# Moving the delta-rule preparation of a gated-DeltaNet layer into the input projection of the same layer

## Chip, cores and metric

The kernel runs on one core of a Trainium2 chip. It is one program in Bass, one launch. The metric is the device time of one execution in microseconds; lower is better. Everything is float32 except the operands of the large projections, which are split into a high and a low float32r part and multiplied in three passes.

## What is computed

A decoder of two layers on 2048 tokens, width 1024. Layer 1 is a gated DeltaNet (8 heads of 128), layer 2 an attention with forget gates (16 heads of 64) over one shared K/V stream. The change is in layer 1 alone:

```python
proj = h @ w_in                                  # 3072 columns q,k,v; 1024 z; 8 a; 8 b
qkv = silu(causal_conv4(qkv, conv_w))
q, k = l2_norm(q), l2_norm(k)                    # per head
beta = sigmoid(b);  g = -exp(a_log) * softplus(a + dt_bias)
g_c = cumsum(g) within a chunk
decay = exp(tril(g_c[i] - g_c[j]))
a_strict = tril((k*beta) @ k.T * decay, -1)      # Gram product of k with k
qk = (q @ k.T) * decay                           # Gram product of q with k
u, w = solve((a_strict + I), [v*beta, k*beta*exp(g_c)])
# then a scan over the chunks with a 128x128 state per head
```

The kernel takes chunks of 128 tokens (16 chunks). Only the 32x32 diagonal blocks of `a_strict + I` are inverted by elimination; larger blocks are joined by matmuls in the scan.

## The kernel before

The program is a row of stages. Each stage (`Stage`) has its own tensors and semaphores and ends with a barrier of all engines; results pass through DRAM. Names carry the stage's prefix: `st` (modulation vectors and first norm), `pa` (projection of layer 1), `da` (delta-rule preparation), `dr` (the scan), `oa` (output projection), `pk`, `pb` (projections of layer 2), `at` (attention), `ob` (output projection).

**Stage pa, `deltanet_projection`.** 33 tiles of 128 output columns by 2048 tokens, in the order 16 of q and k, 8 of v, 8 of z, and one for the 16 gate columns a and b. A tile has four blocks of 512 tokens; a block is 24 matmuls (8 slices of the contraction by three passes, L309 to L311) into one of four PSUM banks. Per tile:

- TensorE: four blocks, each waits for its bank to be free; then, for q and k, the sum of squares of the *previous* tile's result (`norm`, L375: a matmul with ones, after `squared`).
- VectorE: splits the weights of the tile after next (L389, L391), scales the previous q/k tile by its inverse norm (L407, after `rooted`), and convolves this tile in four steps (L415, L418).
- ScalarE: four copies of banks (L473) to `ybuf`, which has two slots; logarithm and exponential of the norms (L477, L479); silu (L484) and square (L488) of the convolved tile.
- GpSimd issues the store of each finished tile (L510, L516, L520, L522): one row of 2048 tokens per partition. SP loads the weights, four tiles at a time.

**Stage da, `delta_prepare`.** First the gates for all tokens on 8 partitions, turned by TensorE into columns (`cols`). Then for each chunk `c`: SP loads q and k of the chunk (`da_qk`, rows of 128 tokens) and the cumulated gates broadcast to 128 partitions (`da_gb`); ScalarE makes the decays (L846, L850, L852); TensorE makes the two Gram products of 8 heads (L874, L879); VectorE multiplies them by the decays into `B` (L810) and `PT` (L816); GpSimd masks the decays (L717) and scales the queries (L725); SP stores `qh`, `PT`, the diagonal blocks of `B` (L644) and its lower blocks (L646, L648). After each four chunks the 128 diagonal blocks of 32x32 come back as one batch (`Bd`), VectorE inverts them by elimination (L779, L782; four parts, one behind each chunk), and SP stores the inverse (L661). All per-chunk tiles have two buffers. `da_qk` is read from what `pa` stored, so the stages cannot overlap.

**Stage dr, `delta_rule`.** The scan; it loads k and v (`dr_kv`), the scaled queries, `PT`, z and the inverse blocks per chunk.

The order within a stage is written out by hand, engine by engine; semaphores tie them together.

## Time and profile before

| | us |
|---|---|
| median of 3 runs | 3893.09 |
| lowest and highest | 3884.18, 3896.68 |
| the profiled execution, its own time | 3891.56 |
| its span in the trace | 3890.1 |
| TensorE busy (share of the span) | 3267.1 (84%) |
| VectorE busy | 1773.0 (46%) |
| ScalarE busy | 1208.4 (31%) |
| GpSimd busy | 635.7 (16%) |

The span is what the trace covers of the execution; the execution's own time is 1.5 us longer. Busy shares are means over stages with different limits. Lines such as L375 are lines of the kernel before; those of the kernel after are named as such. "Releaser" is what ended an engine's idle time.

### The profile page before, as it was taken

Reading aid. Unit: us, or ns where it says so; the run is one execution under the profiler, and the core shown is the slowest. Engines: PE = TensorE matmul, PEld = TensorE weight load, DVE = VectorE, ACT = ScalarE, POOL = GpSimd, SP = SyncE. Lnnn points to the kernel's source line nnn.
Section 4 is the critical chain, followed back from the end, with each engine's and each line's share of the span. In section 5 each row is a group of like instructions: output and inputs, shape, how many; then the busy total and the mean of one; then the engine's idle time right before and its main releaser. Section 6 shows DMA issues by size and latency. Waiting matters only on the chain. (4 is left out here: it accounts for less than half of the span.)

```text
span 3890.1 us, 46371 instructions
## 1 busy us (share of the span) xinstructions
PE 3267.1 (84%) x15538; PEld 2366.5 (61%) x15538; DVE 1773.0 (46%) x2803; ACT 1208.4 (31%) x2088; POOL 635.7 (16%) x669
## 2 busy tenths in 40 slices
PE   4599999999333289979699978998799999999798
PEld 2377777887333278868488857886444444444376
DVE  3545445400345556645522114211667766667443
ACT  2455552111322144522411013121144444334411
POOL 1000000000222255311000000000233333323310
PEclk7799999999566689989799989999699999999899
DMA  9611111111477567455543225421733234230233
GB/s 395 234 65 65 58 61 76 71 70 45 116 186 172 149 184 208 141 184 177 162 120 87 65 83 152 112 88 51 169 99 82 67 74 99 74 99 12 76 130 119
DMA packets 358110, 454.76 MB, mean 117 GB/s; under 512 B 75368, under 2 KB 255912, under 8 KB 348472
## 3 DMA queue, kind: packets, MB, share of 16 engines
q1 hardware_dynamic: 335696, 356.54, 32.4%
q0 software_dynamic: 22224, 95.82, 7.0%
q8 instruction: 103, 1.69, 0.2%
q14 instruction: 87, 0.71, 0.1%
HBM read 291.69 MB, written 160.46 MB: 116 GB/s over the span
## 5 line engine op out<-in xcount | busy, mean ns | idle before, releaser
L2097 ACT ACTIVATE at_probs<-at_logits 128x512 f32<-128x512 f32 (+3 forms) x640 | 334.3, 532 | 469.0 <-PE at_logits L1960 392.0
L309 PE MATMUL pa_y<-pa_h_high,pa_w_high 128*128 128x512 f32 x1056 | 427.3, 405 | 28.2 <-DVE pa_w_low L391 23.3
L1934 DVE TENSOR_REDUCE at_partial<-at_rough 128x1 f32<-128x512 f32 (+1 forms) x600 | 356.0, 607 | 190.3 <-PE at_rough L1925 120.1
L311 PE MATMUL pa_y<-pa_h_high,pa_w_low 128*128 128x512 f32 x1056 | 419.9, 398 | 0.0
L310 PE MATMUL pa_y<-pa_h_low,pa_w_high 128*128 128x512 f32 x1056 | 419.8, 398 | 0.0
L1842 POOL TENSOR_TENSOR at_sum_g<-at_sum_g,at_probs 128x512 f32<-128x512 f32 (+2 forms) x240 | 250.9, 1062 | 418.9 <-ACT at_probs L2097 417.1
L1971 PE MATMUL at_o<-at_probs,at_V 128*64 128x512 f32 (+3 forms) x1280 | 314.6, 571 | 3.5 <-ACT at_probs L2097 3.5
L1957 PE MATMUL at_logits<-at_Q,at_K 67*128 67x512 f32 (+3 forms) x640 | 274.4, 429 | 24.8 <-issue 12.2
L1922 PE MATMUL at_rough<-at_K,at_Q 66*128 66x512 f32 (+1 forms) x600 | 242.8, 411 | 53.9 <-DMA at_K<-s_Fp 51.1
L1960 PE MATMUL at_logits<-at_Q,at_K 128*128 128x512 f32 (+3 forms) x640 | 259.5, 406 | 0.0
L309 PEld LDWEIGHTS pa_y<-pa_h_high,pa_w_high 128*128 128x128 f32 x1056 | 199.8, 189 | 81.9 <-issue 34.1
L309 PE MATMUL pk_y<-pk_h_high,pk_w_high 128*128 128x512 f32 x544 | 218.0, 401 | 31.5 <-POOL pk_ident L98 28.3
L309 PE MATMUL pb_y<-pb_h_high,pb_w_high 128*128 128x512 f32 x512 | 204.9, 400 | 37.4 <-POOL pb_ident L98 32.4
L1957 PEld LDWEIGHTS at_logits<-at_Q,at_K 67*128 67x128 f32 x640 | 126.4, 197 | 179.8 <-ACT at_probs L2097 109.8
L310 PEld LDWEIGHTS pa_y<-pa_h_low,pa_w_high 128*128 128x128 f32 x1056 | 199.8, 189 | 51.9 <-issue 4.1
L311 PEld LDWEIGHTS pa_y<-pa_h_high,pa_w_low 128*128 128x128 f32 x1056 | 199.8, 189 | 48.8
L1922 PEld LDWEIGHTS at_rough<-at_K,at_Q 66*128 66x128 f32 x600 | 121.3, 203 | 162.0 <-DVE at_partial L1934 87.1
L310 PE MATMUL pk_y<-pk_h_low,pk_w_high 128*128 128x512 f32 x544 | 216.8, 398 | 0.0
L311 PE MATMUL pk_y<-pk_h_high,pk_w_low 128*128 128x512 f32 x544 | 216.7, 398 | 0.0
L310 PE MATMUL pb_y<-pb_h_low,pb_w_high 128*128 128x512 f32 x512 | 204.4, 399 | 0.0
L311 PE MATMUL pb_y<-pb_h_high,pb_w_low 128*128 128x512 f32 x512 | 204.3, 399 | 0.0
L874 PE MATMUL da_psG<-da_qk 128*128 128x128 f32 x256 | 59.5, 426 | 159.9 <-DMA da_qk<-s_qkv 110.1
(339 smaller groups left out, 5546.4 us busy)
## 6 DMA issues: line engine op xcount, KB each, us to landing
s_qkv<-pa_sil POOLq DMA_DIRECT2D x25, 1024.0 KB, 4.1
at_Q<-s_Q SPq DMA_DIRECT2D x96, 256.0 KB, 6.1
da_qk<-s_qkv SPq DMA_DIRECT2D x16, 1024.0 KB, 7.1
dr_kv<-s_qkv SPq DMA_DIRECT2D x16, 1024.0 KB
s_K<-pk_parts SPq DMA_DIRECT2D x32, 512.0 KB, 8.0
s_Q<-pb_parts SPq DMA_DIRECT2D x32, 512.0 KB, 8.0
at_K<-s_K SPq DMA_DIRECT2D x32, 512.0 KB, 5.3
pa_wraw<-in_a_w_in_dram SPq DMA_DIRECT2D x7, 2048.0 KB, 7.9
```

The lines of the kernel that those rows point to most:

```text
L309: nc.tensor.matmul(out, w_high[:, k], h_high[:, k], start=k == 0, stop=False)
L310: nc.tensor.matmul(out, w_high[:, k], h_low[:, k], start=False, stop=False)
L311: ins = nc.tensor.matmul(out, w_low[:, k], h_high[:, k], start=False, stop=k == KC - 1)
L874: ins = nc.tensor.matmul(at_head(psG, g, h), k[:, h], k[:, h], start=True, stop=True)
L1842: ins = g.tensor_tensor(sum_g[:, h, off:BLK], sum_g[:, h, off:BLK], x, ALU.add)
L1922: ins = nc.tensor.matmul(bank[:, 0:width], Q1[s][0:DH + 2, h, q_at], K1[s][0:DH + 2, h, grp * BLK:grp * BLK + width], start=True, stop=grp ...
L1934: reduced.done(nc.vector.tensor_reduce(partial[:, h, qb * NQ + sub, grp:grp + 1], rough_bank(j, alone)[:, 0:width], AX.X, ALU.max))
L1957: nc.tensor.matmul(out, K1[s][0:DH + 3, h, k_at], Q1[s][0:DH + 3, h, q_at], start=True, stop=False)
L1960: logits_ok.done(nc.tensor.matmul(out, K2[s][:, h, k_at], Q2[s][:, h, q_at], start=False, stop=True))
L1971: ins = nc.tensor.matmul(o[at, m % 2, off:BLK], V[s][:, kb, at], probs[:, j % 3, h, off:BLK], start=kb == 0, stop=kb == NQ * (qb + 1) - 1)
L2097: probs_ok.done(nc.scalar.activation(probs[:, j % 3, h, off:BLK], logits[:, h, off:BLK], ACT.Exp))
```

## The change

`delta_prepare` is gone as a stage. All it does is now in `deltanet_projection`:

- The gate tile comes first instead of last. Its result goes to DRAM and comes back with one row per (chunk, head) on 128 partitions; the gate arithmetic runs on 128x128 tiles behind tile 14, on VectorE and ScalarE (`gates_first`, `gates_second`).
- From block 0 of tile 18 (the third tile of v) TensorE makes the Gram products of a chunk behind every third block (`step(T, n)` counts blocks from there; chunk `c` at step `3c`). ScalarE's decays are two steps ahead, GpSimd's query scaling one step ahead and its mask one step behind.
- The batches of block inverses are solved from steps 24, 32, 41 and 49 (`SOLVE_AT`).
- To make room, buffers shrink: `ybuf` has one slot instead of two, the weights are loaded for two tiles at a time (by ScalarE's queue), `qk`, `E`, `B`, `PT`, `Bd` and `X` have one buffer each (`qk` lies in `sil`, `E` and `B` in `sq`). Only the gate broadcast keeps two; the scaled queries are written over it.
- The norm of tile T-1 is summed behind block 2 of tile T, not behind block 3.
- Stored q, k, v and z are chunk-major: the store of a tile writes pieces of 128 tokens (512 bytes), and the loads of a chunk, here and in the scan, read one contiguous run per partition.
- Loops over tiles are written out instead of run as loops.

```diff
-            if norm_before:
-                pe.wait_ge(squared, T + 1)
-                for n in range(NB):
-                    ins = nc.tensor.matmul(norm[:, n], ones[:, :], sq[:, n * BLK:(n + 1) * BLK], start=True, stop=True)
-                ins.then_inc(summed, 1)
...
+    SOLVE_AT = {24: 0, 32: 1, 41: 2, 49: 3}
...
+    def step(T, n):
+        return (T - FIRST) * NB + n
+
     with Stage(nc, "pa") as st:
-        ybuf = st.sb("ybuf", [P, 2, 3 + SEQ])
...
+        ybuf, acc = st.sb("ybuf", [P, 3 + SEQ]), st.sb("acc", [P, SEQ])
...
+        qk = sil[:, :].rearrange("p (t j) -> p t j", j=P)
+        E, B = (sq[:, k * AH * P:(k + 1) * AH * P].rearrange("p (h j) -> p h j", j=P) for k in range(2))
...
+            def load_qk(c):
+                if c:
+                    qkg_ok.wait(sp, c - 1, 1)
+                    qh_ok.wait(sp, c - 1, 1)
+                sp.dma_start(qk, s_qkv[c, :, 0:2 * AH]).then_inc(qk_in, 16)
+
+            def load_gb(c):
+                if c >= 2:
+                    sp.wait_ge(qh_stored[c % 2], 16 * (c // 2))
+                sp.dma_start(gbuf[c % 2][:, :, :], s_G[c].unsqueeze(0).to_broadcast([P, AH, P])).then_inc(gb_in[c % 2], 16)
...
+            for c in range(NC):
+                qh_ok.wait(sp, c, 1)
+                sp.dma_start(s_qh[c], gbuf[c % 2][:, :, :]).then_inc(qh_stored[c % 2], 16)
+                if c + 1 < NC:
+                    load_qk(c + 1)
+                store_blocks(c)
+                masked.wait(sp, c, 1)
+                sp.dma_start(s_PT[c], PT[:, :, :]).then_inc(pt_stored, 16)
...
+            for T in range(QK):
+                scaled.wait(pool, T)
+                pool.dma_start(s_qkv[:, :, T].rearrange("c p j -> p c j"), chunk_major(sil[:, :])).then_inc(stored, 16)
+            for T in range(QK, TILES + 1):
+                for n in range(NB):
+                    if n == 0 and T > QK and kind(T - 1) == "z":
+                        bank_free.wait(pool, T - 1, NB - 1)
+                        pool.dma_start(s_z[:, :, T - 1 - QK - V].rearrange("c p j -> p c j"), chunk_major(ybuf[:, 3:])).then_inc(late_stored, 16)
...
+                for n in range(NB):
+                    if T == 0:
+                        pe.wait_ge(ab_free, n + 1)
+                    bank_free.wait(pe, T - 1, n)
+                    bank_full.done(passes(n, T % 2))
+                    if n == 2 and 1 <= T <= QK:
+                        squared.wait(pe, T - 1)
...
+                    if q >= 0 and q % 3 == 0 and q // 3 < NC:
+                        gram(q // 3)
...
+                        if T == QK - 2:
+                            gates_first()
+                            gates_second()
...
+                        if kind(T) != "z" or T == QK + V:
+                            convolved.wait(act, T - 1)
+                        else:
+                            act.wait_ge(late_stored, 16 * (T - QK))
...
+                    if T < QK:
+                        if T:
+                            act.wait_ge(stored, 16 * T)
+                        silu_done.done(a.activation(sil[:, :], acc[:, :], ACT.Silu))
```

What moves on the engines shows best in their own order. ScalarE, one tile of q or k, before (from the last copy of a bank on; a table load brings in the coefficients of another function):

```order
L473 ACTIVATE pa_ybuf<-pa_y 128x512 [waits pa_bank_full]
L477 ACT_TABLE_LOAD
L477 ACTIVATE pa_sq<-pa_norm,pa_eps 128x2048 [waits pa_summed]
L479 ACT_TABLE_LOAD
L479 ACTIVATE pa_sq<-pa_sq 128x2048 [waits pa_act_step]
...
L483 REGISTER_ALU [waits pa_convolved]
L484 ACT_TABLE_LOAD
L484 ACTIVATE pa_sil<-pa_acc 128x2048 [waits pa_stored]
L488 ACTIVATE pa_sq<-pa_sil 128x2048 [waits pa_scaled,pa_silu_done]
```

and the same engine in one tile of q or k of the kernel after:

```order
L801 ACTIVATE pa_ybuf<-pa_y 128x512 [waits pa_convolved,pa_bank_full]
L804 DMA pa_wraw<-in_a_w_in_dram 128x8x256 [waits pa_w_split]
L801 ACTIVATE pa_ybuf<-pa_y 128x512 [waits pa_bank_full] x2
L807 ACT_TABLE_LOAD
L807 ACTIVATE pa_sq<-pa_norm,pa_eps 128x2048 [waits pa_summed]
L809 ACT_TABLE_LOAD
L809 ACTIVATE pa_sq<-pa_sq 128x2048 [waits pa_act_step]
L801 ACTIVATE pa_ybuf<-pa_y 128x512 [waits pa_bank_full]
L818 ACT_TABLE_LOAD [waits pa_stored]
L818 ACTIVATE pa_sil<-pa_acc 128x2048 [waits pa_convolved]
```

The logarithm and exponential moved ahead of the fourth copy, the weight load is now on this queue, and the table load ahead of the silu waits for the previous tile's store instead of for the convolution.

ScalarE of the kernel after behind tile 14, where the gate arithmetic stands (`pa_gb` and `pa_PT` hold the gates there):

```order
L821 ACTIVATE pa_sq<-pa_sil 128x2048 [waits pa_scaled,pa_silu_done]
L761 ACT_TABLE_LOAD
L761 ACTIVATE pa_hcol<-pa_hcol 128x1 [waits pa_abT_in]
L764 ACTIVATE pa_gb<-pa_gb 128x128 [waits pa_gates_dve]
L766 ACT_TABLE_LOAD
L766 ACTIVATE pa_gb<-pa_gb 128x128 [waits pa_gates_act]
L764 ACT_TABLE_LOAD
...
L766 ACT_TABLE_LOAD
...
L768 ACT_TABLE_LOAD
L768 ACTIVATE pa_gb<-pa_gb 128x128 [waits pa_gates_dve]
L770 ACTIVATE pa_PT<-pa_PT 128x128 x3
L801 ACTIVATE pa_ybuf<-pa_y 128x512 [waits pa_convolved,pa_bank_full]
```

Five table loads and nine small activations, two of them behind VectorE's part, now stand ahead of the copies of tile 15; before, nothing stood there.

TensorE of the kernel after at the end of block 0 of tile 18, where the first chunk stands (`pa_norm` is the PSUM of the norms, `pa_sil` holds q and k of the chunk):

```order
L310 MATMUL pa_y<-pa_h_low,pa_w_high 128x512
L311 MATMUL pa_y<-pa_h_high,pa_w_low 128x512
L564 MATMUL pa_norm<-pa_sil 128x128 [waits pa_qk_in,pa_nn_ok]
L564 MATMUL pa_norm<-pa_sil 128x128 x7
L569 MATMUL pa_norm<-pa_sil 128x128 x8
L309 MATMUL pa_y<-pa_h_high,pa_w_high 128x512 [waits pa_bank_free]
```

Sixteen products of one chunk now stand between two blocks of a tile, and the next block waits behind them.

## Rows read from the trace of the kernel before

**Rows 1.** The engines by stretch: q/k tiles; v and z tiles; preparation's chunks; scan.
```profile
core 0: us, PE busy (x) PEld busy (x) DVE busy (x) ACT busy (x) POOL busy (x), PEclk, DMA share, GB/s
194.00:605.00 411.00, 411.00 (x1651) 310.83 (x1650) 199.41 (x112) 217.55 (x178) 8.97 (x16) 1.00 0.16 61
605.00:966.00 361.00, 360.44 (x1538) 289.30 (x1536) 95.61 (x63) 58.09 (x76) 9.53 (x17) 1.00 0.17 67
...
1016.00:1283.00 267.00, 92.68 (x492) 89.75 (x491) 126.21 (x335) 77.08 (x192) 63.88 (x64) 0.64 0.76 176
...
1321.00:1658.00 337.00, 285.37 (x2240) 259.96 (x2240) 186.82 (x570) 150.83 (x353) 156.41 (x115) 0.94 0.63 180
```

**Rows 2.** Waits, 1016 to 1283 us: total us, times, longest us.
```profile
ACT da_E L846 <- DMA da_gb<-s_g: 182.2, 16, 16.1
...
PE da_psG L874 <- DMA da_qk<-s_qkv: 110.1, 11, 12.6
DVE da_B L810 <- DMA s_PT<-da_PT: 92.1, 11, 13.3
```

**Rows 3.** Timeline of ACT and SP at the edges of the removed stage.
```profile
965.48 0.59 ACT L473 ACTIVATE pa_acc<-pa_y 16x512 f32<-16x512 f32 x1 [5.03 <-PE pa_y L311]
...
973.47 0.36 SPq L618 DMA_DIRECT2D da_araw<-s_abT  x1
...
1321.36 1.18 SPq L923 DMA_DIRECT2D dr_M<-s_X  x2
```

**Rows 4.** The stores of q/k tiles (L510), then GpSimd's timeline at z and gate tile.
```profile
L510 POOL DMA_DIRECT2D s_qkv<-pa_sil x16: 541/561/582, 199.8 to 588.0; - x16
...
DMA to landing us min/median/max: 4.1/4.2/4.2
...
943.89 0.53 POOL L520 DMA_DIRECT2D s_zT<-pa_sil  x1 [21.95 <-ACT pa_sil L473]
```

**Rows 5.** Groups of TensorE: f32 products in the scan, in the preparation.
```profile
L1018 PE MATMUL dr_psA<-dr_S,dr_kv 128*128 128x128 f32 x256 | 31.2, 275 | 0.0
...
L874 PE MATMUL da_psG<-da_qk 128*128 128x128 f32 x256 | 59.5, 426 | 159.9 <-DMA da_qk<-s_qkv 110.1 <-DVE da_B L810 47.9 <-DVEq L762 2.0
```

**Rows 6.** Timelines of ACT, DVE, POOL in one q/k tile (start, duration).
```profile
414.97 1.28 ACT L484 ACT_TABLE_LOAD   x1 [11.12 <-DVE pa_acc L418]
416.26 1.92 ACT L484 ACTIVATE pa_sil<-pa_acc 128x2048 f32<-128x2048 f32 x1
418.21 1.92 ACT L488 ACTIVATE pa_sq<-pa_sil 128x2048 f32<-128x2048 f32 x1
...
424.29 1.97 ACT L477 ACTIVATE pa_sq<-pa_norm,pa_eps 128x2048 f32<-128x2048 f32 x1 [0.92 <-PE pa_norm L375]
...
427.58 1.92 ACT L479 ACTIVATE pa_sq<-pa_sq 128x2048 f32<-128x2048 f32 x1
...
429.53 2.29 DVE L407 TENSOR_TENSOR pa_sil<-pa_sil,pa_sq 128x2048 f32<-128x2048 f32 x1 [6.71 <-ACT pa_sq L479]
431.74 1.28 DVE L415 TENSOR_SCALAR pa_acc<-pa_ybuf,pa_taps 128x2048 f32<-128x2048 f32 x1
...
435.67 4.85 DVE L418 SCALAR_TENSOR_TENSOR pa_acc<-pa_ybuf,pa_taps,pa_acc 128x2048 f32<-128x2048 f32 x2 [0.15 <-DVE pa_acc L418]
...
432.57 0.56 POOL L510 DMA_DIRECT2D s_qkv<-pa_sil  x1 [25.08 <-DVE pa_sil L407]
```

**Rows 7.** Window in which two loads of 1 MB in 512-byte pieces run.
```profile
976.00:980.00 4.00, 0.00 (x0) 0.00 (x0) 0.00 (x0) 0.00 (x0) 3.85 (x7) 0.50 1.07 255
```

**Rows 8.** DMA issues: KB each, median us from issue to landing.
```profile
da_qk<-s_qkv SPq DMA_DIRECT2D x16, 1024.0 KB, 7.1
...
da_gb<-s_g SPq DMA_DIRECT2D x16, 512.0 KB, 15.1
s_qh<-da_qh SPq DMA_DIRECT2D x16, 512.0 KB, 13.4
```

**Rows 9.** Small activations of the gates, in ACT's timeline.
```profile
1009.84 0.91 ACT L838 ACTIVATE da_cols<-da_cols 128x128 f32<-128x128 f32 x4 [15.75 <-DVEq L757]
```

**Rows 10.** DVE in the scan's start waits for the inverse blocks (timeline).
```profile
1363.64 0.45 DVE L1140 STREAM_TRANSPOSE dr_MT<-dr_M 128x256 f32<-128x256 f32 x1 [14.19 <-DMA dr_M<-s_X]
```

More of the change, by code:

```diff
@@ new lines, with heads, group, flat @@
+HG = AH // 2
+NC = SEQ // P
+SB = 32
+MW = 9 * P
+BETA, NBEG, EKG, EGL = range(4)
+def heads(g):
+    return range(g * HG, (g + 1) * HG)
+def group(g):
+    return slice(g * HG, (g + 1) * HG)
+def flat(x, g):
+    return x[:, group(g)].rearrange("p h c -> p (h c)")
+def at_head(ps, g, h):
+    return ps[:, g, (h % HG) * P:(h % HG + 1) * P]
+def deltanet_projection(nc, s_xnT, s_mod, a_pre_g, a_w_in, a_conv_w, gate_cols, s_qkv, s_z, s_abT, s_G, s_cols, s_qh, s_PT, s_D,
+                        s_X, s_B5, s_B6):
+    QK, V = 2 * AH, AH
+    TILES = QK + 2 * V
+    FIRST = QK + 2
+    SCALE = float(P) ** -0.5
+    BATCHES = NC // 4
+    SOLVE_AT = {24: 0, 32: 1, 41: 2, 49: 3}
+    def kind(T):
+        return "qk" if T < QK else "v" if T < QK + V else "z"
+    def step(T, n):
+        return (T - FIRST) * NB + n
@@ new lines, in _, with passes, gram @@
+        @block.tensor
+        def _(pe):
+            def passes(n, slot):
+                at = slice(n * BLK, (n + 1) * BLK)
+                return three_passes(nc, y[:, n], w_high[:, slot], w_low[:, slot], h.high[:, :, at], h.low[:, :, at])
+            def gram(c):
+                q, k = qk[:, 0:AH], qk[:, AH:2 * AH]
+                pe.wait_ge(qk_in, 16 * (c + 1))
+                for g in range(2):
+                    b_ok.wait(pe, c - 1, g)
+                    for hd in heads(g):
+                        ins = nc.tensor.matmul(at_head(psG, g, hd), k[:, hd], k[:, hd], start=True, stop=True)
+                    gram_ok.done(ins)
+                for g in range(2):
+                    pt_ok.wait(pe, c - 1, g)
+                    for hd in heads(g):
+                        ins = nc.tensor.matmul(at_head(psQ, g, hd), k[:, hd], q[:, hd], start=True, stop=True)
+                    qkg_ok.done(ins)
+            pe.wait_ge(consts_set, 1)
+            pe.wait_ge(ab_split, 1)
@@ L419, in post @@
[L419 to L430 removed]
+                    ins = v.scalar_tensor_tensor(acc[:, :], x, w, acc[:, :], ALU.mult, ALU.add)
@@ new lines, in convolve, with scale, gates_first @@
+                    steps.did(ins) if j < 3 else convolved.done(ins)
+            def scale(T):
+                rooted.wait(dve, T)
+                scaled.done(v.tensor_tensor(sil[:, :], sil[:, :], sq[:, :], ALU.mult))
+            gates = Steps(dve, gates_dve)
+            def gates_first():
+                dve.wait_ge(abT_in, 48)
+                gates.did(v.tensor_scalar(araw, araw, hcol[:, 1:2], None, ALU.add))
+                gates.wait()
+                gates.did(v.scalar_tensor_tensor(atmp, araw, -1.0, araw, ALU.mult, ALU.max))
+                gates.did(v.scalar_tensor_tensor(btmp, braw, -1.0, braw, ALU.mult, ALU.max))
@@ L433, in _ @@
+            split(1, wab, ab_split)
             dve.wait_ge(w_first, 16)
[L434 to L435 removed]
+            split(0, wraw[:, :, 0:P], w_split)
             h.make(dve, range(KC, NB * KC))
[L437 to L446 removed]
@@ L506, in _ @@
[L506 to L523 removed]
+            gates = Steps(act, gates_act)
```

796 lines of the change are left out of this document (328 added, 468 removed).

## The prediction, as recorded before the changed kernel was run

> **What bounds the kernel now.** I read the windows first: one line per stage, TensorE's busy time beside the clock it was granted. In q/k tiles it is busy throughout at 1.00, the 2.4 GHz level; in v and z tiles as well; in the preparation's chunks it is busy for 93 of 267 us at a mean of 0.64, between its two levels [rows 1]. So the projection is bound by TensorE and the preparation by something else. The waits name it: ScalarE waits 182 us for the gate broadcasts, TensorE 110 us for q and k, VectorE 92 us for the stores of PT, all of them transfers [rows 2]; the DMA engines are 76% busy [rows 1]. In the v and z tiles VectorE has 95.6 and ScalarE 58.1 of 361 us, the DMA engines 17% [rows 1]: that is the room which the change fills. The sum below follows TensorE, and asks at each place whether something else ends later.
>
> **Units.** A v or z tile takes 21.95 + 0.53 = 22.48 us, a block 5.62. A q/k tile takes (588.0 - 199.8) / 15 = 25.88 us, so its norm costs 3.40 [rows 4].
>
> **1. The stage goes.** From the end of the last projection block (released copy at 965.4) to the first load of the scan (1321.4) pass 356.0 us [rows 3]. **-356.0.** Four to be paid again:
>
> **2. New tail.** Before, 8.1 us lie between the last block and the next stage's first DMA [rows 3], with a small store in them. After, the last z store is behind the last block: a bank copy, then 1 MB in 512-byte pieces. Rows of 8 KB land in 4.1 us [rows 4]; in 512-byte pieces the engines move 255 GB/s [rows 7], 4.1 us for the data alone, and such a load lands in 7.1 [rows 8]. I take 6.5, so 3.4 more than now. **+11.5** (bounds 8 and 25). The last batch of inverses does not come later: chunk 15 is at step 45 and ten blocks follow (56 us); stores and batch load take about 22, the elimination 22 + 4, the store 5, in all 53. If it slips, it adds its excess here.
>
> **3. Gram products on TensorE.** 32 instructions a chunk. In the preparation they cost 426 ns in the record at the low clock, in the scan at 1.00 a group of 256 equal ones takes 31.2 us, 0.122 each [rows 5]. They will run between busy blocks, so I take the latter: 3.9 a chunk plus 0.1 for the change of operands, 16 times. **+64.** Six transposes for the gate columns **+1.5**; the norm of ones that opens the loop now falls away, **-3.4**. The gate tile only changes its place.
>
> **4. The q/k tiles lose their slack.** Take t = 0 when the norm of tile T-1 ends, now behind block 2. Logarithm, table load, exponential end at 1.97 + 1.28 + 1.92 = 5.2; block 3 at 5.6; the weight split at 7.6; from the start of the scaling to the end of the convolution 440.52 - 429.53 = 11.0, so 18.7; silu and square 3.9: 22.7 [rows 6]. TensorE has finished three blocks at 3 x 5.62 + 5.62 = 22.5. Before, it had a fourth block before the norm. So at best it waits 0.2 us a tile. But the silu's table load (1.28) now stands behind the store of the tile before: scaled at 9.9, issued 0.75 later [rows 6], landed at about 17.2, loaded at 18.5. The cover is gone to within 0.2 us, and each microsecond by which this store is later costs 1 us in each of 16 tiles. I take 0.6 a tile: **+10** (bounds 3 and 40; the upper one from a landing as late as q and k's 7.1 with its issue at full length). The weights, now asked for at 23.3 and needed at 31.5, have 8 us. On this queue they delay only copies.
>
> **5. The gates behind tile 14.** ScalarE has five table loads of 1.28 and nine small activations of 0.23 [rows 9], and waits for about ten small steps of VectorE (0.3 each, half of them while it would be idle): 11 us, before the copies of tile 15 and the logarithm of the norm. That logarithm has 2.4 us of slack (5.2 against 7.6 above). What is late next is the scaling, the convolution and the square: TensorE waits once. **+8** (bounds 0 and 13).
>
> **6. The chunk loop beside v and z.** TensorE needs 3 x 5.62 + 4.0 = 20.9 us a chunk. The others: VectorE 4 a chunk and 11 a v tile; ScalarE 5 a chunk, up to 2.6 of table loads and, in v tiles, silu; GpSimd 2.5 + 1.2 and its stores. SP sends ten DMAs. Their covers are three blocks of TensorE. The transfers: before, 267 / 16 = 16.7 us a chunk at 76% is 12.7 us of the 16 engines [rows 1]. Weights and stores of a v or z tile take 17% of 22.48, and three quarters of a tile go with a chunk: 2.9. The 512-byte side moves from the load of q and k to the stores, about even. 15.6 of 20.9 is 75%, what the engines stood before, and there a chunk took 16.7 us. The longest ring through single buffers is the gate buffer's: decays 6.2, query scaling 2.5, store 13.4, load 15.1 [rows 8], 37 us for two chunks, against 41.8. So TensorE should bind. For single late transfers I put **+5** (bounds 0 and 50).
>
> **7. The scan.** Its start is crowded by DMA; VectorE waits 14.2 us for inverse blocks once [rows 10]. k, v and z come in long runs now. **-5** (bounds -12 and 0).
>
> Sum: -356.0 + 11.5 + 64 + 1.5 - 3.4 + 10 + 8 + 5 - 5 = -264.4. The profiled execution took 3891.6, 1.5 us below the median: 3627.
>
> **A rule against the trace.** The store of a q/k tile is issued by GpSimd while VectorE runs the first step of the convolution (432.57, inside 431.74 to 433.02) [rows 6], and all 16 landed in 4.1 to 4.2 us [rows 4], the same as the z stores beside an idle VectorE. So here VectorE costs them nothing, and term 4 stands. The Trainium skill, SBUF — State Buffer, section "SBUF: two separate sides", says otherwise of such DMAs: VectorE can lock GpSimd out of their shared port, so that it cannot write the descriptors, and the transfer sits until the VectorE instruction ends. In the trace only 128 rows had to be described; with 2048 pieces the writing lasts longer and could meet the lock. That is rival C.
>
> **Rivals.**
> A. *The store in q/k tiles is late.* It lands at 19 to 20 instead of 17.2; 1.5 to 2.5 us a tile, +24 to +40 in place of +10: 3641 to 3657. For: a margin of 0.2 us. Against: 4.2 us is steady.
> B. *Transfers bind the chunk loop.* At 24 us a chunk instead of 20.9 it costs 16 x 3.1 = 50: 3672. For: the broadcast's 15.1 and SP's single queue, where a late step holds all behind it (mask, batch store, next q and k). Against: the preparation alone ran at 16.7.
> C. *VectorE locks out the descriptors.* The store is issued only when the convolution ends, at 18.7, lands at 25.2, and silu and square end at 30.4: TensorE waits 7.9 us in 16 tiles, +126 in place of 10: 3743. This is the way the page's rule would make it come out.
> D. *Slower than before.* Not by a sum of mishaps but by the gate buffer's ring: it needs two chunks in 41.8 us. The two landings, 28.5 together, bind above 33; to eat the whole gain a chunk must take 20.9 + 264/16 = 37.4, so 66 us for the two. At 70 us a chunk takes 39.4: 3923. For: gate, queries and q/k share one queue. Against: that is 2.5 times what they took at the same load.
>
> **Chances.** Forecast 0.53 (its own range 3605 to 3650), A 0.17, B 0.20, C 0.05, D 0.02; 0.03 is left for what I did not see on the same side. The likeliest case gives 3627. Low end 3602: terms 4 to 6 near their lower bounds, the scan near its own. High end 3700: takes in A and B, and B with a late tail. A measurement of this kernel tells about 0.3%, 12 us, from no change. Faster by more 0.97, within 0.01, slower 0.02.
>
> **What would show it.** The first load of the scan near 1057. Windows: v and z tiles take about 427 us, TensorE busy throughout at 1.00. The waits: TensorE for the square after silu, under 1 us a tile, and once about 8 near tile 15; nothing long for q and k of a chunk. The period of the q/k stores about 26.5. Wrong if: that period is over 27 (A, or over 30, C: then the store's landing, counted from the scaling, tells); a chunk's period is over 22 (B, D), with TensorE waiting for a load; the elimination is still running when the last block ends (tail). If TensorE's clock falls in the new stretch, term 3 is too small.

## The result and the profile after

| | before | after |
|---|---|---|
| median of the runs shown with the result | 3889.01 us (4 runs) | 3598.41 us (4 runs) |
| lowest and highest | 3884.18, 3896.68 | 3591.21, 3610.34 |
| profiled execution | 3891.56 | 3596.84 |

The ratio is 0.926, 95% interval 0.924 to 0.928. The forecast was 3627 with a range of 3602 to 3700: the direction and most of the size are right, but the time lies 3.6 us under the range, so the forecast failed at its low end. Against its own base, the profiled execution, the forecast of 3627.2 is 30.4 us too high.

The windows of the changed kernel, by stretch: q/k tiles up to the gates, the two tiles that hold the gates, the v and z tiles with the chunks, and the tail. They answer to [rows 1].

```profile
core 0: us, PE busy (x) PEld busy (x) DVE busy (x) ACT busy (x) POOL busy (x), PEclk, DMA share, GB/s
241.40:579.10 337.70, 337.29 (x1353) 254.63 (x1353) 160.87 (x92) 177.33 (x143) 21.31 (x13) 1.00 0.22 63
579.10:639.70 60.60, 54.91 (x209) 40.00 (x209) 27.82 (x28) 37.11 (x37) 3.05 (x2) 0.94 0.19 54
640.00:1032.00 392.00, 390.78 (x1938) 324.64 (x1936) 245.96 (x457) 160.94 (x287) 102.84 (x88) 1.00 0.63 190
1032.10:1045.10 13.00, 0.00 (x1) 0.00 (x0) 2.70 (x9) 0.60 (x1) 1.16 (x1) 0.60 0.57 122
```

The third line is the change: TensorE is busy for 390.8 of 392 us at 1.00, the 2.4 GHz level, while the transfers stand at 63% and VectorE at 246 us. The work that took 267 us at a clock of 0.64 now lies beside the v and z tiles. In the second line TensorE is idle for 5.7 us, and its clock is below full.

The stores of the q/k tiles (they answer to [rows 4]), their landing, and the products of k with k by chunk (first and last start stand in the row):

```profile
L534 POOL DMA_DIRECT2D s_qkv<-pa_sil x16: 1387/1663/1668, 241.4 to 639.7; - x16
```
```profile
s_qkv<-pa_sil POOLq DMA_DIRECT2D x16, 1024.0 KB, 6.5
...
pa_gb<-s_G SPq DMA_DIRECT2D x16, 512.0 KB, 6.2
s_qh<-pa_gb SPq DMA_DIRECT2D x16, 512.0 KB, 3.9
```
```profile
L564 PE MATMUL pa_norm<-pa_sil x16: 272/275/275, 663.8 to 665.5; 128*128 128x128 f32 x16
...
L564 PE MATMUL pa_norm<-pa_sil x16: 271/275/275, 972.1 to 973.8; 128*128 128x128 f32 x16
```

Before the gates the stores come at 241.4 and 579.1 with 13 periods between them, so a period is 25.98 us; the median is 25.92, and one is 26.87. [Rows 4] gave 25.88. A chunk takes (972.1 - 663.8) / 15 = 20.55 us on average; a chunk without a wait takes 20.44, and the two with a wait of TensorE 21.29 and 21.14. The gate broadcast lands in 6.2 us instead of 15.1, the scaled queries in 3.9 instead of 13.4 [rows 8]. With the new layout but in the old stage (experiment 2) they still took 14.1 and 14.7, so it is not the layout that shortens them.

One whole q/k tile, ScalarE and VectorE, beside [rows 6]:

```profile
456.14 1.28 ACT L818 ACT_TABLE_LOAD   x1 [10.46 <-DMA s_qkv<-pa_sil]
457.62 1.92 ACT L818 ACTIVATE pa_sil<-pa_acc 128x2048 f32<-128x2048 f32 x1 [0.20 <-DVE pa_acc L640]
459.57 1.92 ACT L821 ACTIVATE pa_sq<-pa_sil 128x2048 f32<-128x2048 f32 x1
...
446.94 2.29 DVE L645 TENSOR_TENSOR pa_sil<-pa_sil,pa_sq 128x2048 f32<-128x2048 f32 x1
449.14 1.28 DVE L637 TENSOR_SCALAR pa_acc<-pa_ybuf,pa_taps 128x2048 f32<-128x2048 f32 x1
450.46 7.13 DVE L640 SCALAR_TENSOR_TENSOR pa_acc<-pa_ybuf,pa_taps,pa_acc 128x2048 f32<-128x2048 f32 x3
```

The table load starts when the store before it has landed (456.14), and ends 0.2 us before the convolution does (457.59). That is the margin of 0.2 us of step 4. It does not hold in every tile. In the tile with the long period the store landed after 7.5 us instead of 6.5; the table load ended 0.8 us behind the convolution, and TensorE waited 0.4 us:

```profile
404.57 1.28 ACT L818 ACT_TABLE_LOAD   x1 [11.42 <-DMA s_qkv<-pa_sil]
...
397.94 7.12 DVE L640 SCALAR_TENSOR_TENSOR pa_acc<-pa_ybuf,pa_taps,pa_acc 128x2048 f32<-128x2048 f32 x3
```

Stage by stage, from first event to first event: the scan 352.1 before and 343.0 after, the attention (which no line of the change touches) 957.3 and 949.8, all between and behind within 1.9 us in sum.

### The profile page after: what moved, and what is told of

Same layout as the page of the kernel before. It is cut to its first block and busy times, and to the rows that moved or that the text cites. A ratio compares the mean times of both kernels' runs of the same rounds, so it can differ in the third digit from the quotient of the medians.

```text
span 3595.3 us, 45723 instructions
## 1 busy us (share of the span) xinstructions
PE 3215.7 (89%) x15502; PEld 2319.9 (65%) x15502; DVE 1758.8 (49%) x2795; ACT 1233.5 (34%) x2112; POOL 674.8 (19%) x666
## 5 line engine op out<-in xcount | busy, mean ns | idle before, releaser
L1922 PE MATMUL at_logits<-at_Q,at_K 67*128 67x512 f32 (+3 forms) x640 | 272.5, 426 | 28.1 <-issue 13.1
L2001 DVE TENSOR_TENSOR at_sum_v<-at_sum_v,at_probs 128x512 f32<-128x512 f32 (+3 forms) x288 | 163.2, 606 | 51.4 <-ACT at_probs L2062 51.2
```

What stands on the lines that cost most here:

```text
L1922: nc.tensor.matmul(out, K1[s][0:DH + 3, h, k_at], Q1[s][0:DH + 3, h, q_at], start=True, stop=False)
L2001: ins = v.tensor_tensor(to, to, x, ALU.add)
```

## The experiments

Four kernels ran in the first group, four in the second, four in the third, each group on one chip beside the kernel before. Some of the texts on record call a chunk 20.67 us; counted from first product to first product it is 20.55.

**1. The norm behind block 3 again.**

```diff
-                    if n == 2 and 1 <= T <= QK:
+                    if n == 3 and 1 <= T <= QK:
```

> The changed kernel with the norm of the tile before summed behind block 3 of a q/k tile, as it was before the change, instead of behind block 2. Theory (term 4): the 26.23 us of a q/k tile (store to store, without the gates' stall of 4.9) hold 0.35 us of waiting that the earlier place of the norm causes; with the fourth block back as cover the period returns to 25.9 and the stall of the gates (term 5) goes, since the logarithm has 5.6 us more. 15 x 0.35 + 4.9 = 10 us: about 3588, and the first load of the scan at 1035. Rival: the 0.35 us has another cause (single buffers, weights in loads of two tiles): no change, 3598, with the stall of 4.9 still there. Other side: ScalarE now copies bank 0 of the next tile only after silu and square, at 20.9 of 26 us; if the weights that are asked for behind that copy come late, VectorE starts late and the period rises above 26.2.

Measured 3595.9 us (5 runs; ratio to before 0.926, 0.923 to 0.929). The period up to the gates is 25.9, as without the edit. So there was nothing to win per tile: the 26.23 of the expectation was the loss at the gates, spread over the tiles. The first load of the scan came at 1041.5, 3.6 us earlier: 2 of them at the gates (58.5 us between the two stores around them instead of 60.6), 0.9 in the 13 periods before, where no period is longer than 26.2; the rest was not traced. The theory fell, and the rival's reading (no loss in a regular tile from the norm's place) stands; what the earlier place costs is about the one tile with a late store.

**2. The layout alone, in the kernel before.** q, k, v and z chunk-major.

```diff
-                pool.dma_start(s_qkv[bass.ds(T * P, P), :], sil[:, :]).then_inc(stored, 16)
+                pool.dma_start(s_qkv[:, :, bass.ds(T, 1)].rearrange("c p t j -> p c (t j)"), chunk_major(sil[:, :])).then_inc(stored, 16)
```

> The kernel before with one part of the change alone: q, k, v and z are stored chunk-major (512-byte pieces in the store, one run per partition in the loads of the preparation and the scan). Theory (term 7, resized after the result): the scan, from its first load to the next stage, becomes 9 us shorter, as it did in the changed kernel; the preparation, which waits for transfers, 5 to 25 us shorter; the projection stays (two slots of ybuf cover 6.5 us of landing), the attention too. Together 3864 to 3880. Rival: the scan's 9 us do not come from the layout (then its stage takes 352 as before), and the preparation is bound by the number of transfers and not by their pieces: 3889.

Measured 3864.2 us (5 runs; 0.993, 0.991 to 0.996). The preparation, from TensorE's last product of the projection to the scan's first load, took 345.4 us instead of 356.3, the scan 345.8 instead of 352.1. The stores of the projection land in 6.1 us, and its period stays 25.9. The trace thus shows 17 us for the layout where the preparation is a stage of its own. The scan's 9 us of the expectation were too many, 6 came; the preparation's 11 lie in its 5 to 25. The medians differ by 25 (3889 and 3864), 8 more than the trace explains, and that remainder stays open; in this profile the attention is 10 us *longer* than in that of before (see 10).

**3. The old layout in the changed kernel.**

```diff
-                pool.dma_start(s_qkv[:, :, T].rearrange("c p j -> p c j"), chunk_major(sil[:, :])).then_inc(stored, 16)
+                pool.dma_start(s_qkv[T * P:(T + 1) * P, :], sil[:, :]).then_inc(stored, 16)
```

> The changed kernel with the old layout of q, k, v and z: rows of 2048 tokens are stored, the chunk's loads read 512-byte pieces. Theory: the stores of q/k tiles land in 4.2 instead of 6.5 us, and that changes nothing in the period (26.2 without the gates' stall), because silu waits for the convolution after it; the tail behind the last block is 2 us shorter, the scan 9 us longer (352), the chunk loop stays bound by TensorE at 20.67 us a chunk. Together 3605. Rival for the layout in the chunk loop: the loads of q and k take as long as before (7.1 us and more) and TensorE waits for them: a chunk over 21 us, 3610 or more. Rival for the store: the period falls to 25.9, so the store did cost 0.35 us a tile: 3600.

Measured 3617.9 us (5 runs; 0.930, 0.928 to 0.933). The stores land in 4.6 us and the period is 25.9 still: in a regular tile of the changed kernel the store costs nothing, and the 13 periods together are 0.7 us shorter, the one late store. The scan took 351.0. A chunk takes 20.83 instead of 20.55 on average. A regular one is 20.44 in both kernels; the difference lies in two chunks, 23.72 and 22.75 here, where TensorE waits 3.1 and 2.1 us for q and k. The expectation of 3605 fits the profiled execution (3604.4), which was the fastest of five; the median is 13 us above it, and no trace shows why. The four profiles with rows have scans of 350.0 to 352.1 (the kernel before, this one, and the two under 8 and 11), the ten with chunk-major layout 343.0 to 346.2. Step 7 is settled: the layout gives the scan about 6.5 us.

**4. The store of q/k tiles later, by two GpSimd instructions.**

```diff
                 scaled.wait(pool, T)
+                for k in range(2):
+                    padded.done(g.affine_select(out=X[:, :, :], in_=X[:, :, :], compare_op=ALU.is_gt, fill=0.0, base=0,
+                                                pattern=[[1, SB], [-1, SB]], channel_multiplier=0))
+                    padded.wait(pool, 2 * T + k + 1)
```

> The changed kernel with two additional GpSimd instructions of 1.27 us each in front of each of the 16 stores of q/k tiles: the store is issued about 2.7 us later. It measures the cover of the store (rival A of the prediction). Theory: ScalarE's table load ends 0.8 us before the convolution does, so 0.8 us are covered and the rest is paid in each tile: 16 x (2.7 - 0.8) = 30 us, a period of 28.1, about 3629. Rival: TensorE has more cover than that (the table load is not what the tile waits for): under 5 us. Other rival: each microsecond is paid in full, +43, 3641, if the table load itself was the last thing.

Measured 3701.6 us (3 runs; 0.953, 0.950 to 0.956): 103 us more than the changed kernel, more than either theory allowed. One tile of it, GpSimd and then the windows behind:

```profile
437.03 5.49 POOL L538 TENSOR_SCALAR_AFFINE_SELECT pa_X<-pa_X 128x1024 f32<-128x1024 f32 x2 [26.20 <-DVE pa_sil L652]
...
442.82 1.17 POOL L541 DMA_DIRECT2D s_qkv<-pa_sil  x1 [0.30 <-POOL pa_X L538]
```
```profile
445.00:450.00 5.00, 4.63 (x20) 3.39 (x18) 2.04 (x1) 1.05 (x1) 0.00 (x0) 1.00 0.65 188
450.00:455.00 5.00, 0.86 (x1) 0.50 (x2) 0.00 (x0) 4.96 (x6) 0.00 (x0) 0.83 0.28 51
455.00:460.00 5.00, 5.00 (x7) 2.02 (x6) 0.00 (x0) 1.83 (x3) 0.00 (x0) 0.50 0.46 159
```

Two things were not in the expectation. The instructions took 2.7 us each instead of 1.27, since they stand beside VectorE's convolution, so the store was issued 5.8 us later and not 2.7. And TensorE, after a wait of 4.5 to 5.2 us, ran at 0.50 (1.2 GHz) for the next stretch: before the gates a period grew by 7.1 us on average (33.10 instead of 25.98), not by the length of the wait. The cover is 0.2 us and not the 0.8 of this expectation, and the price of what goes over it was too low.

**12. The same with one instruction** (from the third group, told here because it belongs here).

```diff
-                for k in range(2):
+                for k in range(1):
```

> The changed kernel with one additional GpSimd instruction ahead of each store of q/k tiles, where two of them (2.71 us each beside VectorE's work instead of 1.27) cost 6.9 us a tile: a stall of TensorE of about 5 and about 2 of half clock behind it. Theory: the store is 2.9 us later less 0.5, as its own record gets shorter; 0.2 are covered: TensorE waits 2.2 us a tile. If low clock comes behind every stall in proportion (2 for 5), the period is 25.93 + 2.2 + 0.9 = 29.0, 3647; if a stall of this length leaves the clock at 1.00, 28.1, 3633. Rival: below 1 us a tile, if the cover is more than 0.2.

Measured 3627.0 us (3 runs; 0.932, 0.929 to 0.935). The instruction took 2.24 us; a regular period is 27.48, 1.6 more than 25.92, and one is 30.27. Both values of the theory (28.1 and 29.0) were too high, the rival's (below 1 us a tile) too low. Waits of TensorE from 244 to 574 us here, then in experiment 4:

```profile
PE pa_norm L594 <- ACT pa_sq L828: 17.1, 12, 2.1
```
```profile
PE pa_norm L594 <- ACT pa_sq L828: 46.0, 10, 5.2
```

Behind waits of 1.3 to 1.9 us TensorE's clock stands at 1.00, and they are paid once. The longest, 2.1 us, is the exception: low clock follows it, and this is the period of 30.27. The waits of 4.6 us are all paid with low clock on top.

The added instruction is not a pure delay of the store, for it slows VectorE as well: the last three steps of the convolution take 7.99 us here and 8.85 in experiment 4, instead of 7.13. The table load still ends last (0.8 us behind the convolution here, 3.2 in experiment 4), so the store's chain sets the wait. But a part of the 1.6 us would have come from the longer convolution alone; the two were not separated. The window behind the wait of 2.1 us, and the three steps:

```profile
418.00:422.00 4.00, 3.56 (x5) 1.50 (x6) 0.00 (x0) 3.12 (x5) 0.00 (x0) 0.58 0.80 244
```
```profile
462.61 7.99 DVE L647 SCALAR_TENSOR_TENSOR pa_acc<-pa_ybuf,pa_taps,pa_acc 128x2048 f32<-128x2048 f32 x3
```

**5. A chunk per two blocks.**

```diff
-    SOLVE_AT = {24: 0, 32: 1, 41: 2, 49: 3}
+    SOLVE_AT = {12: 0, 22: 1, 31: 2, 40: 3}
...
-                    if q >= 0 and q % 3 == 0 and q // 3 < NC:
-                        gram(q // 3)
+                    if q >= 0 and q % 2 == 0 and q // 2 < NC:
+                        gram(q // 2)
```

> The changed kernel with a chunk of the preparation per two token blocks instead of three (the decays one block ahead, the batches of inverses at steps 12, 22, 31 and 40). TensorE's own work is the same, so if nothing else binds, the time is too. Per chunk TensorE now needs 2 x 5.62 + 3.8 = 15.05 us instead of 20.67, and the transfers of a chunk, 63% of 20.67 = 13.0 us of the 16 DMA engines, would fill 86% of it. It measures how far the change stands from rival B. Theory: TensorE still binds, a chunk takes 15.1 to 15.5, the whole 3598 to 3605. Rival B: the transfers bind at the 16.7 us a chunk that the preparation took alone, 16 x 1.65 = 26 us more: 3625, with TensorE waiting for q and k or the gate broadcast, and a further loss where the wait makes its clock fall.

Measured 3632.9 us (4 runs; 0.934, 0.932 to 0.936). The first products of chunks 0 and 15, and TensorE's longest waits:

```profile
L566 PE MATMUL pa_norm<-pa_sil x16: 272/275/275, 663.8 to 665.5; 128*128 128x128 f32 x16
...
L566 PE MATMUL pa_norm<-pa_sil x16: 421/421/582, 926.6 to 929.9; 128*128 128x128 f32 x16
```
```profile
PE pa_norm L566 <- DMA pa_sil<-s_qkv: 18.4, 6, 8.3
...
PE pa_norm L566 <- DVE pa_sq L690: 15.4, 2, 11.2
```
```profile
813.33 3.57 PE L566 MATMUL pa_norm<-pa_sil 128*128 128x128 f32 x16 [11.25 <-DVE pa_sq L690]
```

A chunk takes (926.6 - 663.8) / 15 = 17.52 us where TensorE needs 2 x 5.62 + 3.6 = 14.8, so 41 us are lost in the loop. A loss of the size of rival B exists, then, between 14.8 and 20.55. It is not an even one: six of the fifteen chunks took 14.8 to 14.9 us, and the longest took 26.3. In that one TensorE waited 11.2 us for VectorE (last row), which had elimination steps and the whole convolution of a tile to do before the products of the chunk. In six others TensorE waited for q and k, 18.4 us in all; single buffers can be a reason, since q and k may be loaded only when the last product and the query scaling have read them, but no kernel with second buffers was run. The capacity of the DMA engines, which the expectation named, does not look like the limit: they stand at 73% in the middle of the loop (700 to 900 us), and chunks of 14.8 are shorter than the 16.7 at which transfers should bind. At the end of the loop the products took 421 ns, the low clock again.

**6. The gates spread over two tiles**, where ScalarE waits for the store anyway: the exponentials and logarithms behind the norm's exponential of tile 14, the last four exponentials behind that of tile 15.

```diff
                         rooted.done(a.activation(sq[:, :], sq[:, :], ACT.Exp, scale=-0.5))
+                        if T == QK - 2:
+                            gates_first()
+                        if T == QK - 1:
+                            gates_second()
...
-                if T == QK - 2:
-                    gates_first()
```

> The changed kernel with the gates' activations put where ScalarE waits anyway: the exponentials directly behind the exponential of the norm in tile 14, then the two logarithms (one table load), the last four exponentials behind the norm's exponential of tile 15; VectorE's steps follow in tiles 13, 14 and 15. Between the first store of q and k before the gates (579.1) and the last one (639.7) pass 60.6 us in the changed kernel, two periods of 25.93 and 8.7 us that the gates cost. Theory: ScalarE has 10 us a tile in which it waits for the store before it, so the 8.7 us go: 51.9 between these stores, 3590. Rival: the gates' chain of small steps, or something else at this place, holds TensorE anyway: 60 us, 3598. Since a stall is also paid with low clock behind it, no middle value is expected unless a short stall is left.

Measured 3594.8 us (4 runs; 0.924, 0.922 to 0.926). Two tiles with the gates in them:

```profile
578.90:630.90 52.00, 52.00 (x211) 39.31 (x210) 27.06 (x25) 29.22 (x27) 3.10 (x3) 1.00 0.22 63
```

52.0 us instead of 60.6, TensorE without a gap and at 1.00: the whole 8.6 us go. The first load of the scan comes at 1036.6, 8.5 us earlier. The median fell by 3.6 only, and the profiled execution by 3.1: in it the attention took 957.2 us and not 949.8 (see 10), which ate most of the gain.

**7. Another tail.**

```diff
-    SOLVE_AT = {24: 0, 32: 1, 41: 2, 49: 3}
+    SOLVE_AT = {24: 0, 32: 1, 40: 2, 48: 3}
...
+            def store_z_part(T, m):
+                at = slice(3 + m * BLK, 3 + (m + 1) * BLK)
+                pool.dma_start(s_z[m * BLK // P:(m + 1) * BLK // P, :, T - QK - V].rearrange("c p j -> p c j"), chunk_major(ybuf[:, at])).then_inc(late_stored, 16)
```

> The changed kernel with another end of the projection: the inverses of batches 2 and 3 begin one step earlier (40 and 48), where GpSimd has no query scaling ahead of them, and the last z tile is stored in four parts of 512 tokens as its blocks are copied. From TensorE's last instruction to the first load of the scan pass 13 us in the changed kernel. Theory: both the last z store (ends about 1040.5) and the store of the last batch's inverses (1035.1 + 5.8 = 1040.9) hold the end; with both earlier the tail is about 9 us, 4 less: 3594. Rival 1: the last batch's elimination is not earlier (it waits for its load, behind the store of the batch before): tail 12 to 13. Rival 2: the end is set by neither but by the barrier: 13.

The edges of the tail in the changed kernel (ScalarE's last copy, the last z store, the store of the last inverses, the scan's first load), and then here:

```profile
1032.14 0.60 ACT L801 ACTIVATE pa_ybuf<-pa_y 128x512 f32<-128x512 f32 x1 [5.02 <-PE pa_y L311]
...
1033.06 1.16 POOL L539 DMA_DIRECT2D s_z<-pa_ybuf  x1 [20.02 <-ACT pa_ybuf L801]
...
1035.10 5.82 SPq L459 DMA_DIRECT2D s_X<-pa_Bd  x4
...
1045.11 1.20 SPq L889 DMA_DIRECT2D dr_M<-s_X  x2
```
```profile
1025.21 2.75 SPq L459 DMA_DIRECT2D s_X<-pa_Bd  x4
...
1031.80 0.75 POOL L534 DMA_DIRECT2D s_z<-pa_ybuf  x1 [4.12 <-ACT pa_ybuf L812]
...
1036.71 1.21 SPq L900 DMA_DIRECT2D dr_M<-s_X  x2
```

From the last product's start to the scan pass 6.2 us instead of 13.4: 7 us, not the 4 expected. The inverses of the last batch are stored 10 us earlier, and the last part of z is a quarter of the data. How much each of the two edits gives was not measured. In the changed kernel the elimination did end behind TensorE, by 2.9 us; step 2 had put it ahead. The total, however, was 3605.4 us (4 runs; 0.927, 0.925 to 0.930), no better than the changed kernel, with 975.6 us of attention in the profile.

**8. The norm behind block 2, in the kernel before.**

> The kernel before with one part of the change alone: the norm is summed behind block 2 instead of block 3 of the next tile. Everything else is as before (two slots of ybuf, rows of 2048 tokens in the stores, the preparation as a stage). Theory: the q/k period stays within 0.1 us of 25.9, as it did in the changed kernel: 3889. Rival: 0.3 us a tile or more, 3894, and TensorE waits for the square. It also is a third sample of a kernel with the old preparation for the attention stage, which no edit touches: 957 and 967 us in the two seen, 948 to 950 in the four kernels with the new one. If that is chance, this one may be near 949; if it hangs on the program, 957 or more.

Measured 3919.7 us (4 runs; 1.008, 1.005 to 1.010). This edit, nearly free in the changed kernel, costs 27 us here: the period is 27.6. The theory (25.9) fell; the rival (0.3 us a tile or more) came true with 1.7. ScalarE in one tile:

```profile
455.58 1.28 ACT L483 ACT_TABLE_LOAD   x1 [12.36 <-DVE pa_acc L418]
456.88 1.92 ACT L483 ACTIVATE pa_sil<-pa_acc 128x2048 f32<-128x2048 f32 x1
```

The table load stands *behind* the convolution (its last step ends at 455.49), in the changed kernel beside it. The reason is the loop. ScalarE's instructions with the waits that they carry, in the changed kernel and then in the loop of this one:

```
L818 ACT_TABLE_LOAD [waits pa_stored]
L818 ACTIVATE pa_sil<-pa_acc 128x2048 [waits pa_convolved]
...
L482 REGISTER_ALU [waits pa_convolved]
L483 ACT_TABLE_LOAD
L483 ACTIVATE pa_sil<-pa_acc 128x2048 [waits pa_stored]
```

Written out, the waits are constants, one on the table load and one on the silu. In the loop their values are computed in a register, and the wait for the convolution sits on the instruction that computes the next value, ahead of the table load. Add three waits of 0.15 us between VectorE's steps [rows 6], which only the loop has, and 1.28 + 0.45 = 1.7 is about the difference (27.6 against 25.9). Experiment 11 tests the first part.

**11. The two waits in the other order**, otherwise as 8.

```diff
-            act.wait_ge(convolved, T + 3)
             act.wait_ge(stored, 16 * (T + 1))
+            act.wait_ge(convolved, T + 3)
```

> The kernel before with the norm behind block 2, where a q/k tile took 27.6 us, and with the two waits ahead of ScalarE's silu in the other order: the wait for the convolution now stands on the silu itself and the table load waits only for the store of the tile before, as it does in the changed kernel, whose loops are written out. Theory: the table load (1.28 us) leaves the chain and runs beside the convolution; the period falls from 27.6 to 26.3, what is left being the three waits of 0.15 between VectorE's steps that only the loop has. 16 x 1.3 = 21 us less than with the norm alone: 3899. Rival: the 27.6 has another cause, the period stays: 3920.

Measured 3902.6 us (10 runs; 1.004, 1.002 to 1.005). ScalarE in a regular tile:

```profile
524.72 1.28 ACT L483 ACT_TABLE_LOAD   x1 [8.66 <-DMA s_qkv<-pa_sil]
528.45 1.92 ACT L483 ACTIVATE pa_sil<-pa_acc 128x2048 f32<-128x2048 f32 x1 [2.45 <-DVE pa_acc L418]
```

The table load has left the chain, and a regular tile takes 26.2 us. One tile in four still takes 28 to 29.7. It is the one in which SP loads the weights of four tiles:

```profile
222.14 0.41 SPq L363 DMA_DIRECT2D pa_wraw<-in_a_w_in_dram  x1
...
233.46 1.28 ACT L483 ACT_TABLE_LOAD   x1 [12.86 <-DMA s_qkv<-pa_sil]
```

The store of that tile, issued at 224.96 beside these 2 MB, lands after 8.4 us instead of 4.2; the table load, which now waits for it, ends 1.9 us behind the convolution, and TensorE waits 1.8 us. This is rival A's mechanism, in a kernel with the old loop. By the medians 17 of the 21 us came; between the traces of 8 and 11 the last block of the projection moved by 13.5 us (995.5 to 982.0).

**10. The changed kernel once more.**

> The changed kernel once more, to the letter, on the same chip as the other three of this group. It gives a second profile of the same program. Theory (the attention stage varies from run to run): its projection and scan are within 1 us of the first profile (first load of the scan 1045, scan 343 to 346) and its attention stage differs from 949.8 by up to 25 us in either direction. Rival (it goes with the program): 949 to 951 again.

Measured 3601.7 us (5 runs; 0.928, 0.925 to 0.931). First load of the scan at 1045.5, scan 343.3, attention 952.9. The same program gives 949.8 and 952.9, and over all 14 profiles the same attention code took 947.0 to 975.6 us, in both families: 957.3, 966.9, 955.0 and 948.9 with the old preparation, 947.0 to 957.2 eight times and 974.0 and 975.6 with the new. The windows of that stage in experiments 7 and 11:

```profile
2441.50:3417.10 975.60, 888.48 (x3849) 438.46 (x3849) 636.52 (x1118) 376.50 (x716) 296.43 (x313) 0.90 0.32 82
```
```profile
2748.60:3697.50 948.90, 866.28 (x3848) 429.32 (x3848) 635.86 (x1118) 377.18 (x716) 297.55 (x313) 0.93 0.33 84
```

ScalarE's busy time is the same and VectorE's within 2%; TensorE's granted clock differs, 0.90 and 0.93, and with it its busy time. What makes it fall more often in one execution than in another stays open.

**9. Gates and tail together.**

> The changed kernel with both edits that shortened the projection: the gates' activations spread over tiles 14 and 15 behind the norm's exponential, and the earlier last batches with the last z store in four parts. The first load of the scan came at 1045.1 in the changed kernel, at 1036.6 and 1036.7 with one edit each. Theory: they add up, since they lie at different places on TensorE's path: 1028 to 1029, and the whole is 16 us less than the changed kernel. But the attention stage, which no edit touches, varied from 947 to 976 us between the profiles; the total can only show the 16 us if that is the chance of a single run. So: 3582 in the median; rival: 3590 to 3600, if the attention stage of a program goes with the program.

Measured 3586.8 us (6 runs; 0.923, 0.920 to 0.926), against 3601.7 (0.928, 0.925 to 0.931) of the changed kernel in the same group. The first load of the scan comes at 1028.3: the two gains add up to 17 us in the trace. Of the six runs four took 3580 to 3588, two 3605 and 3609; the profiled one is of the two, with 974.0 us of attention. The 15 us between the medians fit the 17 of the trace; the intervals of the two ratios overlap a little, so the total alone does not prove it.

## Why the forecast failed, and what of it held

The working follows the steps of the prediction; forecast, then what the profiled execution shows.

| step | forecast | measured |
|---|---|---|
| 1, the stage goes | -356.0 | -356.0 |
| 2, tail | +11.5 | +13.0 |
| 3, Gram products and transposes | +65.5 | +58.8 |
| 3, norm of ones | -3.4 | -3.4 |
| 4, q/k tiles | +10 | +1.3 |
| 5, gates | +8 | +8.8 |
| 6, chunk loop | +5 | +1.8 |
| 7, scan | -5 | -9.1 |
| stages behind the scan | 0 | -9.4 |
| start of the projection | 0 | -0.7 |
| sum | -264.4 | -294.9 |

The profiled executions differ by 3891.56 - 3596.84 = 294.7. Step 3 is (20.44 - 16.86) x 16 = 57.3, with the transposes left at the 1.5 of the forecast; the norm of ones is left at its forecast too. Step 4 is (25.98 - 25.88) x 13, step 5 60.6 - 2 x 25.88, step 6 (20.55 - 20.44) x 15; the projection starts at 155.0 instead of 155.7. Of the signs that the prediction named, the first load of the scan came at 1045.1 (forecast 1057), the q/k period is 26.0 (26.5), and TensorE's long wait at the gates is 4.9 us (about 8).

- **Step 4 is the term of the sum that failed most**, by 8.7 of the 30 us. It stood at +10 with a lower bound of 3, and 1.3 was measured; its mechanism is right and its size is not. The 0.6 us a tile were made of a wait of 0.2 that every tile should have and of an allowance of 0.4 for stores that come late. The first did not come: the 11.0 us from scaling to convolution's end were read in the loop of the kernel before and hold its three waits of 0.15 [rows 6]; here they are 10.65 (446.94 to 457.59), and TensorE does not wait in a regular tile. The second came in one tile of 16, where it cost 0.7 us. That the margin of the table load came out as the 0.2 of the prediction is luck: the shorter convolution took 0.35 us from it, and the store, issued 0.3 us behind the scaling instead of 0.75, gave 0.4 back.
- **The stages behind the scan** stood at nothing, without a reason, and gave 9.4 us, 7.5 of them in the attention. The spread of that stage, up to 29 us between profiles, is wider than the whole margin of my low end; my range had nothing for it. The low end of 3602 had step 4 near its bound of 3 already. What carried the time below it are the terms that had no bound at all: this one, and step 3 with 6.7 us.
- **Step 6**, another allowance without a row, was 5 us, and 1.8 were measured: TensorE waited 1.2 us in two chunks. In both, SP's queue held the load of q and k back behind a batch's store of inverses (one was issued at 879.2 where its turn was at 872.0, and landed after 10.2 us, the longest of the 16). So SP's single queue, rival B's argument, is seen at work, at a small price. Experiment 5 shows that the limit is not far off.
- **Step 3**: 3.6 us a chunk instead of 4.0. The products start 0.113 us apart (663.8 to 665.5), not 0.122, and the 0.1 for the change of operands was not there.
- **Step 5** came out right for a reason that the prediction did not have: the stall is 4.9 us (the row below: total, times, longest) with 0.8 of another behind it, and low clock costs the rest; the second window of the first fence shows 0.94. This is luck in part.

```profile
PE pa_norm L587 <- ACT pa_sq L821: 5.3, 2, 4.9
```

- **Step 7** was too small, within its bound of -12; the layout is worth 6.5 us there (experiments 2 and 3). The other 2.6 lie within the spread of that stage, 343.0 to 346.2.
- **Step 2** was 1.5 us short, and two larger misses hide in that. In experiment 5, where the last inverses are stored long before, the last z store alone gives a tail of 9.3 us (1073.8 to 1083.1), 2.2 less than forecast. In the changed kernel the last elimination ended behind TensorE and not ahead of it: the inverses landed at 1043.3, 4 us behind z, and set the 13.0.
- **Rival A** is real as a mechanism: with 0.2 us of cover it cost 0.7 us in the one tile with a late store, it costs one tile in four of experiment 11 about 1.8, and in experiment 12, where the table load ends 1.8 us later, a regular tile pays 1.6; long delays are paid with low clock besides (experiment 4).
- **Rival C** did not occur as the prediction had it: no store waited for the end of the convolution. But the issue does wait for the end of one step. In a regular tile it begins 0.90 us before the end of the convolution's first step (L637, 1.28 us long) and takes 1.66; in one tile it begins 0.63 before that end and takes 1.39; in experiment 2 it begins 0.45 before and takes 1.21 (first row below). Beside the later steps it takes 1.17 (experiment 4, second row), in a v tile, which does not meet the first step, 1.20 (third row). So it ends 0.76 us behind the first step, and 0.45 us is what that costs; the landing is 6.5 us instead of 6.1. The Trainium skill, SBUF — State Buffer, section "SBUF: two separate sides", gives the lock to one VectorE instruction, and by these stores the trace agrees; the prediction had stretched it over all four steps. The section has the lock also between a VectorE instruction with two inputs in SBUF and a GpSimd instruction that reads SBUF, and the trace agrees in experiments 4 and 12: the last row, of experiment 4, has 2.19 to 3.19 us where the same instruction takes 1.27 alone, and VectorE's steps beside it grew too.

```profile
L513 POOL DMA_DIRECT2D s_qkv<-pa_sil x16: 1152/1208/1211, 199.8 to 588.1; - x16
```
```profile
L541 POOL DMA_DIRECT2D s_qkv<-pa_sil x16: 1170/1171/1184, 244.6 to 746.0; - x16
```
```profile
L542 POOL DMA_DIRECT2D s_qkv<-pa_acc x8: 1154/1196/1205, 650.0 to 839.9; - x8
```
```profile
L538 POOL TENSOR_SCALAR_AFFINE_SELECT pa_X<-pa_X x32: 2185/2712/3189, 238.9 to 742.5; 128x1024 f32<-128x1024 f32 x32
```

- **Rival D** was far off: the gate buffer's two landings took 10.1 us together, not 28.5.

## What to carry to other kernels

When a transfer-bound stage can be laid beside TensorE-bound work, its landings shrink too: do not carry its crowded landing times over to the new place. Give an allowance for lateness only where a row shows a spread, and put the spread of the untouched stages into the range instead. Price a chain for the changed kernel from a row without the waits that the change removes. And where a chain closes to within tenths of a microsecond, look at which instruction carries which wait: a table load that waits for the wrong thing is worth 1.3 us in every tile, and writing a loop out can move it.

## What the runs showed that I had not expected

- A stall of TensorE is paid with low clock behind it when it is long. Waits of 4.6 us on average cost about 7.1 in all (experiment 4), and the gates 8.8 for 5.7 of idle time; waits of 1.3 to 1.9 us leave the clock at 1.00, and the one of 2.1 us had 0.58 behind it (experiment 12).
- Writing out the loop moved ScalarE's table load from behind the convolution to beside it; without that, by experiments 8 and 11, the earlier norm would have cost about 1.7 us a tile. The prediction got this right by reading the changed code, and never saw that it hung on the unrolling.
- A GpSimd instruction of 1.27 us takes 2.19 to 3.19 beside VectorE's convolution and lengthens the convolution by about 0.86; used as a delay it is not a measure.
